# High halves of attention outputs by ScalarE and low halves by VectorE out of the bank, fewer idle products, a new order and layout in the state-space stage

## What is computed

```python
# layer 0
u, q = split(rms_norm(x) @ w_in, [768, 256])
# S5: 48 groups of 16 channels, 64 complex states each
lam_bar = exp(lam * dt); b_bar = ((lam_bar - 1) / lam)[..., None] * b
bu = einsum('gpn,bsgn->bsgp', b_bar, u)
states = associative_scan(s_t = lam_bar * s_(t-1) + bu_t)
y = einsum('gnp,bsgp->bsgn', c, states).real + d_skip * u
g = gelu(y); s5 = g * sigmoid(g @ w_glu + b_glu)
x = x + concat(s5, memory_attention(q, mem)) @ w_out
x = x + (silu(h @ w_gate) * (h @ w_up)) @ w_down          # h = rms_norm(x)
# shared K, V once; layer 1
x = x + concat(moba_attention(12 heads), memory_attention(4 heads)) @ w_out
# router: top 2 of 8 experts of width 3584
x = x + moe_swiglu(rms_norm(x))
```

## Time and profile before

| | us |
|---|---|
| median of 3 runs | 1474.73 (1473.92 to 1476.48) |
| the profiled execution | 1474.49 |
| its span | 1472.8 |
| TensorE busy | 1439.1 |
| VectorE busy | 1191.7 |
| ScalarE busy | 978.0 |
| GpSimd busy | 100.2 |

### The profile page before, as it was taken

One profiled execution on the slowest core, in us unless ns is written; L12 is line 12 of the kernel. 1 busy time (PEld: TensorE's weight loads), 2 busy tenths in 40 slices (PEclk: granted clock), 3 DMA queues, 4 the chain that ended last, 5 costly groups with the idle time before them and its releaser, 6 DMA issues.

```text
span 1472.8 us, 20745 instructions
## 1 busy us (share of the span) xinstructions
PE 1439.1 (98%) x7832; PEld 1209.2 (82%) x7832; DVE 1191.7 (81%) x1190; ACT 978.0 (66%) x954; POOL 100.2 (7%) x130
## 2 busy tenths in 40 slices
PE   8989999999989999999999999999999999999997
PEld 4678799998869888888888888888888888888886
DVE  6895455555777988988898898888889889888887
ACT  5326444444674777877777777787787777778775
POOL 1753100000240000000000000000000000000000
PEclk9999999999999999999999999999999999999999
DMA  8437655443326999999999999999999999999992
GB/s 230 145 71 260 236 192 185 147 155 115 121 109 233 349 370 371 331 362 375 337 351 360 348 357 366 378 323 363 373 337 358 366 343 349 370 373 331 359 376 94
DMA packets 193088, 425.95 MB, mean 289 GB/s; under 512 B 14002, under 2 KB 23088, under 8 KB 192944
## 3 DMA queue, kind: packets, MB, share of 16 engines
q1 hardware_dynamic: 192480, 424.35, 80.3%
q10 hardware_dynamic: 560, 0.94, 0.3%
HBM read 421.67 MB, written 1.05 MB: 287 GB/s over the span
## 4 chain that ended last, share of the span: by engine, by line
PE 91%; ACT 2%; POOL 1%; DVE 1%; issue 1%; ACTq 1%; DMA 1%; SPq 1%; DVEq 0%
PE bank L425 78%; PE bank L447 3%; PE bank L908 2%; PE bank L490 2%; PE bank L920 1%; PE bank L700 1%; PE bank L529 1%; PE bank L453 1%; ACTq L1021 1%; SPq L1081 1%; POOL work L1171 1%; ACT w_hi L1531 1%; DMA ring<-work 1%; PE bank L626 1%; DVE ring L1697 0%
## 5 line engine op out<-in xcount | busy, mean ns | idle before, releaser
L2015 DVE TENSOR_TENSOR w_lo<-ring,w_hi 128x2048 fp32r<-128x2048 f32 x341 | 777.7, 2290 | 99.6 <-ACT w_hi L1531 98.2
L1531 ACT ACTIVATE w_hi<-ring 128x2048 fp32r<-128x2048 f32 x341 | 649.1, 1917 | 129.1 <-PE bank L425 126.1
L425 PE MATMUL bank<-w_hi,xg_hl 128*128 128x512 f32 x1792 | 557.1, 392 | 0.0
L425 PEld LDWEIGHTS bank<-w_hi,xg_hl 128*128 128x128 f32 x1792 | 332.8, 188 | 67.2
L425 PE MATMUL bank<-w_lo,xg_hl 128*128 128x512 f32 x896 | 349.4, 390 | 0.0
L425 PE MATMUL bank<-w_hi,at_hl 128*128 128x512 f32 x896 | 277.5, 391 | 0.0
L425 PEld LDWEIGHTS bank<-w_lo,xg_hl 128*128 128x128 f32 x896 | 168.2, 188 | 35.8
L425 PEld LDWEIGHTS bank<-w_hi,at_hl 128*128 128x128 f32 x896 | 167.1, 188 | 33.9
L425 PE MATMUL bank<-w_lo,at_hl 128*128 128x512 f32 x448 | 174.5, 389 | 0.0
L1888 DVE TENSOR_TENSOR fpart_hl<-ring,fpart_hl 128x1024 fp32r<-128x1024 f32 x66 | 80.6, 1224 | 75.1 <-ACT fpart_hl L1439 74.9
L425 PE MATMUL bank<-ht_hl,fpart_hl 128*128 128x256 f32 x1056 | 128.0, 283 | 0.0
(11 more groups left out here) (253 smaller groups left out, 1151.7 us busy)
## 6 DMA issues: line engine op xcount, KB each, us to landing
ring<-in_l_moe_w_gate SPq DMA_DIRECT2D x58, 2048.0 KB, 8.0
ring<-in_l_moe_w_up SPq DMA_DIRECT2D x57, 2048.0 KB, 7.9
ring<-in_l_moe_w_down SPq DMA_DIRECT2D x56, 2048.0 KB, 7.9
ring<-in_l_ffn_w_gate SPq DMA_DIRECT2D x5, 2048.0 KB, 9.0
ring<-in_l_ffn_w_up SPq DMA_DIRECT2D x5, 2048.0 KB, 7.9
ring<-in_l_ffn_w_down SPq DMA_DIRECT2D x5, 2048.0 KB, 7.5
ring<-in_l_w_in SPq DMA_DIRECT2D x4, 2048.0 KB, 9.3
ring<-in_l_w_out SPq DMA_DIRECT2D x4, 2048.0 KB, 8.7
```

The lines of the kernel that those rows point to most:

```text
L425: last = mm(p, lhsT=xs[a], rhs=ws[b], start=start and q == 0, stop=stop and q == 2, **kw)
L1531: ac(w_hi(n), at(e_slot(q) * SLOT + j * HALF, HALF), ACT.Copy).then_inc(S("hi"), 1)
L2015: tt(LO[e_slot(q)][:, j * HALF:(j + 1) * HALF], at(e_slot(q) * SLOT + j * HALF, HALF), w_hi(n).bitcast(fp), ALU.subtract).then_inc(S("lo"), 1)
```

## The change

It has these parts; lines are those of the kernel before.

- VX holds the chunks in the order (r b): chunk b * 4 + r lies at r * 8 + b, so a pass over the blocks reads and writes neighbours. ScalarE permutes when it copies Ug out of the bank; the last activation puts the order right. The copies into Xbd are split in two by this.
- Tm lies over Wt instead of Bm, Kst, Ysb and Xbd over Bm. Half of Tm is cleared by GpSimd after CA, the other by ScalarE before V's copies; Xbd is cleared by ScalarE, half before K's copies, half before its DMAs.
- The D term is 24 products into K's banks; GpSimd's addition is gone. K's products wait for CA piece by piece. Carried products (L678) come before the Toeplitz ones (L670).
- VectorE's powers come before its wait for V, the squares of q0 after the scan.
- The high half of an attention output is made by ScalarE (`o_hi`) and the low half by VectorE (`o_lo`), both from the bank; `o_out` and `o_halves` are gone. In layer 0 the second pair's halves stand between the second and third weight half.
- The high halves of `wout1b` are made before the pairs.
- Idle products: 8 to 5 after the router, 7 to 3 after the placing.

```diff
-        Tm = at(18432, 2, STEPS * PAIRS * GDIM)
+        Tm = at(B0, 2, STEPS * PAIRS * GDIM)
...
+                pe.wait_ge(S("s5_ca"), 2 * jq + 2)
...
+                for a in range(4):
+                    mm(kb[jq // 4][32 * a:32 * a + 32, c0:c0 + GDIM], lhsT=ident[0:32, 0:32], rhs=MD[:, jq * 4 + a],
+                       start=False, stop=True, skip_group_check=True)
...
-                    pe.wait_ge(S("m0_ct"), k - 5)
+                    read_out(pe, ("m0", "O", k - 6))
...
-                pe.wait_ge(S("a1_ct"), k + 1)
+                read_out(pe, ("a1", "O", k))
...
-            idle_products(6, 8)
+            idle_products(6, 5)
...
-            idle_products(7, 7)
+            idle_products(7, 3)
...
-            got(pool, ("V", 2))
-            g.memset(Tm, 0.0).then_inc(S("tm_zero"), 1)
-            g.memset(Xbd, 0.0).then_inc(S("xbd_zero"), 1)
-            for n in range(2):
-                read_out(pool, ("K", n))
-            g.tensor_tensor(Kst[:, 0], Kst[:, 0], MD, ALU.add).then_inc(S("kst_d"), 1)
+            got(pool, ("Bm", 11))
+            g.memset(Tm[:, 1], 0.0).then_inc(S("tm_zero"), 1)
...
-                    free(ac(Ug[:, n * 4:n * 4 + 16], p[:, :].rearrange("p (a c) -> p a c", a=16), ACT.Copy), ("Ug", n // 4))
+                    free(ac(Ug[:, n * 4:n * 4 + 16].rearrange("p a (r b) -> p a r b", r=SL),
+                            p[:, :].rearrange("p (a b r) -> p a r b", a=16, r=SL), ACT.Copy), ("Ug", n // 4))
...
+            def o_hi(tag, n, dst, heads):
+
+                p = got(act, (tag, "O", n))
+                ac(dst[:, heads[2 * n][4]], p[:, 0:T], ACT.Copy).then_inc(S(tag + "_o_hi"), 1)
+
...
-            XB = VX.rearrange("p i j (b r) -> p (i j) b r", r=SL)
+            XB = VX.rearrange("p i j (r b) -> p (i j) r b", r=SL)
...
-                carry(0, 0, SB, XB[:, :, :, r - 1], XB[:, :, :, r])
+                carry(0, 0, SB, XB[:, :, r - 1], XB[:, :, r])
...
+            def o_lo(tag, n, dst, low, heads):
+                dve.wait_ge(S(tag + "_o_hi"), n + 1)
+                k = heads[2 * n][4]
+                free(tt(low[:, k], PS[units[(tag, "O", n)][0]][:, 0:T], dst[:, k].bitcast(fp), ALU.subtract), (tag, "O", n))
```

More of the change, by code:

```diff
@@ L127, in trunk @@
         Wt = at(B0, 2, PAIRS, P)
-        Kst = at(B0, STEPS, PAIRS, GDIM, rows=32)
+        Kst = at(18432, STEPS, PAIRS, GDIM, rows=32)
         U4 = at(18432, STEPS, MAIN, rows=CHUNKS)
@@ L660, in _ @@
             proj_kv("memkv1", MT[1], "mkv1", (6, 7))
+            yb = [unit(pe, ("Y", n), n) for n in range(3)]
+            pe.wait_ge(S("xbd"), 12)
+            for n in range(3):
+                for a in range(4):
+                    for ri in range(2):
+                        for jh in range(2):
+                            j = 8 * n + 4 * jh + a
+                            mm(yb[n][64 * jh:64 * jh + 64, a * P:(a + 1) * P], lhsT=Xbd[:, ri, j], rhs=CA[:, ri, j],
+                               start=(a == 0 and ri == 0), stop=False, skip_group_check=True)
             pe.wait_ge(S("tm"), 16 * 16)
-            yb = [unit(pe, ("Y", n), n) for n in range(3)]
             for n in range(3):
@@ L1015, in toeplitz @@
         def toeplitz(eng, g2):
-            eng.wait_ge(S("kst_d"), 1)
-            eng.wait_ge(S("tm_zero"), 1)
+            for n in range(2):
+                read_out(eng, ("K", n))
+            eng.wait_ge(S("tm_zero"), 2)
             Kr, row = Kst.rearrange("p k j o -> p (k j o)"), PAIRS * GDIM
@@ L1228, in _ @@
             root("q1b", 2, hss[:, 24:40], hrs[:, 24:40], HD)
-            for n in range(8):
-                o_halves("a1", n, HTHL[:, 0], n, HTHL[:, 1])
             root("f1", 2, ss[:, 0:2], rs[:, 0:2], D)
@@ L1765, in next_powers @@
                 link(tt(power_rows(w0 + step + 1, n), t0_, t1_, ALU.add))
-            for n in range(3):
-                read_out(dve, ("V", n))
             read_out(dve, "q_pw")
```

94 lines of the change are left out of this document (48 added, 46 removed).

## The result

The changed kernel takes 1460.21 us (median of 4 runs, 1458.43 to 1460.66) for 1474.76 of the kernel before (4 runs): a ratio of 0.990, 95% interval 0.988 to 0.991. It is 14.5 us faster, where 6.8 was forecast. The profiled execution took 1460.04 us, with a span of 1458.3 and a mean granted clock of 0.996; before it was 1474.49, 1472.8 and 0.991.

The account below looks back on a forecast made before the run. TensorE, busy 98% of the span, bounds the kernel; wins come only where it waits or runs at half clock. 0.7 + 3.0 + 1.5 + 1.4 = 6.6 us off 1474.73 gives 1468.1, set to 1467.9; range 1463.5 to 1471.9.

Parts of the forecast that it names:

- State-space stage: Layer 0's state-space stage: faster carry passes and earlier powers end it at 116.5, 0.7 us won (2.7 won to 3.4 lost).
- Who is late next: ScalarE.: State-space stage: ScalarE's DMA issue and four carried-state copies end at 104.7, after VectorE's at about 102.9.
- ScalarE's issue: State-space stage: ScalarE's DMA issue starts at about 91.4, as before, and ends at about 102.7.
- The clock: State-space stage: carried products start at half clock, which returns between 107 and 110.5, costing 2.0 us more.
- at nothing, at most 0.3 us: State-space stage: D's 24 products on TensorE and K's products following CA in pieces are covered.
- The Toeplitz products: End of the state-space stage: the Toeplitz products keep their 4.3 us, at 44 ns each.
- Memory attention's halves: End of the memory attention: halves straight from the bank remove a 1.97 us wait and a clock fall; 3.0 us won.
- The pairs: Layer 1's pairs: 1.95 us won at the end, first pairs lose 1.2, later ones regain 0.8; 1.5 us won.
- Idle products: Router: fewer idle products gain 2.3 us, the gather loses 0.9 at half clock; 1.4 us won.
- Rival A: State-space scan gets no faster, since the broadcast operand, not the stride, costs the factor two; time 1472, chance 14%.
- C: Rival: layer 1's pairs make TensorE wait on ScalarE and the clock drops; kernel slower, 1477 to 1495, chance 4%.
- B: Rival: all terms at their good ends, clock up for carried products and gather; 10.4 us won, 1464.3, chance 18%.

Follow-up runs that it names:

- e11: Changed kernel with only the high weight halves of the second output block (wout1b) back in layer 1's pairs; 1464.77 us, ratio 0.9932 to the kernel before.
- e19: Changed kernel with eight and seven idle products at the router and eight instead of twelve at the program's start; 1460.14 us, ratio 0.9896.
- e2: Changed kernel with the state-space layout of the kernel before (strided carry passes); 1468.05 us, ratio 0.9959.
- e6: Changed kernel with VectorE's squares of q0 put back ahead of V; 1463.85 us, ratio 0.9923.
- e12: Changed kernel without the 24 products that add D to K, so the result lacks the D term; 1461.72 us, ratio 0.9922.
- e16: Kernel before with only VectorE's squares of q0 moved behind the scan; 1471.45 us, ratio 0.9986.
- e9: Changed kernel with the memory attention's output halves made as before, by GpSimd from VectorE's copy; 1464.09 us, ratio 0.9936.
- e10: Changed kernel with layer 1's pairs as before: GpSimd makes the output halves, weight halves come in the pairs; 1462.75 us, ratio 0.9926.
- e7: Changed kernel with eight and seven idle products at the router, as in the kernel before; 1459.13 us, ratio 0.9898.
- e13: Second run of the changed kernel with eight and seven idle products at the router; 1459.61 us, ratio 0.9897.
- e17: Kernel before with only the router's idle products changed, to five and three; 1473.34 us, ratio 0.9995.
- e18: Kernel before with only the new state-space layout (contiguous carry passes); 1474.18 us, ratio 1.0002.
- e4: Changed kernel with ScalarE's eight Toeplitz DMAs held until its own last clear is done; 1463.67 us, ratio 0.9935.
- e3: Changed kernel with the Toeplitz products again ahead of the carried ones; 1461.92 us, ratio 0.9906.
- e5: Kernel before, unedited, run again for a second profiled execution; 1475.10 us, a single run.

## Why the prediction failed

**State-space stage.** "Scan end: 101.4", "Who is late next: ScalarE.", carried products at 104.8, end at 116.5. Measured: 98.4, the two threads within 0.3 us, 100.48, 108.74. The missing 7.8 us are in four pieces; the first is luck, the other three are errors.
- *V's start, 3.2 us, luck of the traces.* The forecast was worked out from an execution with V at 76.45, and the profiled execution of the changed kernel had it at 73.22. With V late (e11, at 76.81) the passes ended at 101.45, as forecast, ScalarE's issue was the later thread, as forecast, and the carried products began at 104.02, and at 103.93 in e19. On the averages the stage won 8.0 us for 0.7 forecast: of the 7.3 missing, 1.9 are V's start (mean 74.55), 1.0 that the stage ended earlier in the one trace of the kernel before than it does on average, and the rest the three errors.
- *ScalarE's issue, 1.1 us.* The step that failed is "So its issue starts at about 91.4, as before". I had read ScalarE's idle 1.2 us as clears alone and kept them and the query copies ahead of the DMAs. The traces show the addition of D on GpSimd as the releaser in the kernel before, and the issue running beside ScalarE's own copies in the changed one. It started at 86.81 and ended at 98.1 instead of 102.7. Of these 4.6 us V's start is 3.2; counted from V's start the issue began after 13.6 us (13.9 in e11, 14.3 in e19) for a forecast of 15.0, and the carried products after 27.2 to 27.7 for 28.4.
- *The clock, 2.0 us.* I charged them because the clock "has then fallen". TensorE had to stand for 3.9 us in my plan and stood 0.54. The size was right: the carried products took 7.31, 8.29 and 7.13 us for 5.46 in the runs where it did fall (e2, e6, e12), 1.7 to 2.8 more. It was the event that did not come. The first step has only 1.1 of the 3.4 us that the stand lost. The other 2.3 are TensorE's own: K's products with D among them (six steps, 7.0 us for 4.3) put the projection's start 12.7 us behind V's for 10.5. I had costed them "at nothing, at most 0.3 us" (e12: 1.8 us), and here that error hid a stand.
- *The Toeplitz products, 1.5 us.* 2.83 us for 4.30. I had written that these 44 ns each came "with no step at the clock's return" and kept them. At 2.4 GHz throughout they take 29 ns each; the row of before held a mixture.

The squares of q0 I took to be hidden by V's products. They were in front of the powers, and with V early also of the scan, which ended 2.4 us later with them in the old place (e6, 100.8 and the carried products at 102.92). In e11 and e19, with V late, VectorE waited 0.80 and 2.16 us for V all the same, so there part or nearly all of the 2.4 us would have been hidden. In the kernel before, where they delay K, the step is worth 2 to 3 us (e16).

**Memory attention's halves.** Right: 3.4 for 3.0, wait and clock both (e9). Ahead of it 0.4 were lost, as in the working.
**The pairs.** Right in mechanism, 2.2 for 1.5 (e10, e11). By the starts of L655 against those of before, the lead fell from 11.85 to 10.97 in the first three pairs (0.9 lost, 1.2 forecast) and was 12.19 at the sixth (1.2 back, 0.8 forecast); the wait at the end gave the rest.
**Idle products.** 1.2 for 1.4 in the first pair of traces, by two errors that cancel: the gather ran at half clock nearly throughout, which the forecast had named as a sign of being wrong, and lost 1.9 us and not 0.9; the stretch ahead of it won 3.0 and not 2.3. And e7, e13 and e17 do not bear out that the counts won it. This term was not shown; what e17 and e10 have in common with e7 is only a clock that was up for the gather.
**Rival A** has fallen (e2), **C** did not come: the waits in the first pairs are 0.57 and 0.65 us and the clock stays. **B**, all terms at their good ends, 1464.3, was the nearest case, and still 4 us short, because its bound for the stage kept the 104.8 for the carried products and the 4.3 us for the Toeplitz ones.

## What to carry to other kernels

When two threads end together at a wait, a step that shortens one can be worth nothing alone (e18) and its full price once the other is shorter too (e2: 7.3 us, where the passes alone were costed at 5.8): write down for each thread when it would end if the other took no time, and cost every edit against both. What holds a DMA queue is the semaphore that its issue waits for, so look for the instruction that ends just before the issue starts, on any engine. A half-clock charge that was put on a wait has to be redone when the plan shortens the wait, together with the slow rows of whatever ran behind it; it stays uncertain even so (a stand of 2.19 us without a fall in e4, of 2.22 with one in e12). And a forecast that counts from one trace carries that execution's start with it: here 3.2 us came from there, so count each step from the event that releases it.

## What the runs showed of the hardware

- DMA issues on ScalarE's queue began while a copy of that engine had just started and another copy and a clear were still to run (86.81 against 89.2), and the first of the eight issues took 0.62 us and the second 1.76, where the other six took 1.48 each.
- In the first powers (L1772 on after, 96 elements, twice) VectorE took 1.24 us, in e16 0.43 for the same pair. In the first GpSimd was in one of its additions (0.7 us each) until 78.74, in e16 in a memset. The Trainium skill ("SBUF — State Buffer", SBUF: two separate sides) says that a VectorE instruction with two SBUF inputs blocks only against a GpSimd one that reads SBUF, for its full length; 0.8 us more beside additions and none beside a memset agree.
- The 24 idle passes at the start took 2.94 us in ten of the 18 profiled executions that had them and 4.6 to 5.2 in the other eight, with a granted clock shown as 1.00 in both. The first projection then begins at 14.0 to 14.7 or at 15.1 to 16.4. Neither kernel edits this.
- With the stand of 0.5 us before the first product of layer 0's gate the same, the 12 products behind it (L704, in the kernel before L700) took 2.83 us in most runs and 4.3 to 4.5 in six of them (e3, e4, e5, e6, e11, e19): a fall of the clock that comes some 5 us after the stage in some executions and costs 1.5 to 1.7 us.
